# Loading the second weight slab in halves and asking for the rotary and bias tables behind it, at the entry of a long kernel

## The chip, the cores and the metric

The kernel runs on one core of one Trainium2 chip. The time is device microseconds of one execution of the whole program; lower is better. A core has a matrix engine (TensorE, PE in the profile; its weight loads are PEld), a vector engine (DVE), a scalar engine (ACT), GpSimd (POOL), a sequencer for DMA (SP), and 16 DMA engines that all queues share.

## What is computed

The reference is a chain of residual layers on 256 tokens of width 1024, in float32. Two layers of a first model (axial-rotary grouped-query attention beside dilated attention with a bias table, then an MLP; latent attention, then an MLP) are followed by two of a second model (gated MLP, differential attention, gated MLP; gated MLP, retention, gated MLP). Only the entry of the first layer matters here:

```python
hn = rms_norm(h, norm_mix_g[0])
proj = hn @ ab_w_in[0]
qa, ka, va, qb, kb, vb = jnp.split(proj, split_ab, axis=-1)
qa = rms_norm(qa.reshape(b, s, A_HEADS, HEAD_DIM), a_q_norm_g[0])
ka = rms_norm(ka.reshape(b, s, A_KV_HEADS, HEAD_DIM), a_k_norm_g[0])
qa = apply_rope(qa, cos_ax, sin_ax)
ka = apply_rope(ka, cos_ax, sin_ax)
...
biases.append(rel_bias[t5_bucket(off)].astype(jnp.float32).T)
```

## The kernel before

Weights come from memory as slabs of 128 x 2048 float32 (1 MB). The ring `raw` holds six of them. SP asks for slab n + 6 once slab n has been split. The split turns a slab into a high part `whi` (a cast by ACT, `split_high`, L241) and a low part `wlo` (raw minus high, by DVE, `split_low`, L245), each with a ring of three. The activations are split in the same way into `xh` and `xl`, both in the tile `xhl`. A product is then three matmuls: high with high, high with low, low with high. TensorE takes the slabs in the order in which they lie in memory. Every engine's program is written out by hand, and only semaphores tie the engines together, so each engine runs its list strictly in order.

The entry of the kernel:

- **SP** (L2675 to L2680) asks for the first 128 rows of x, the first half of slab 0, the other 128 rows of x, the second half of slab 0, then slabs 1 to 5 whole.
- **ACT** (`raw_scalar`, q = 0) casts the first half of slab 0, scales a block of transposed x (`first_side`), casts the second half, scales two more blocks, casts slab 1 whole (L241), and then squares x for the norm (L510). Before all of that, at L2781, it asks for the rotary table `tabs` (128 x 256, 128 KB) once the first rows of x have landed.
- **DVE** (`norm_vector`, q = 0) makes the low parts of x (`first_rest`, L549) and of the halves of slab 0 (`first_low`, L233), then the low part of slab 1 (L245).
- **TensorE** transposes x (L498), multiplies with slab 0 in pieces (`first_block`, L395), then with slab 1 (`second_slab`): for each half t of the tokens, 16 matmuls with the high part of the slab (L430, L431), behind a wait for `hi_ready`, and 8 with the low part (L434), behind a wait for `lo_ready`. Next are the bias table (`table_tensor`, L1381, which waits for `rel_loaded`), a spread of the norm factors (L754), slab 2 (`project_tokens`, L260 to L262), and after its first 24 matmuls the transposition of the rotated keys (`turn_kind(0)`, L1039), which waits for DVE's `ab_roped`.
- **POOL** asks for the gains of the rotary table (`rope_rows`, L2702, which land in `tabs` too) when the first rows of x have landed, and for the bias tables when the second have: `rel_sb` (L2704, 16 KB), `hot_sb` (L2706, 64 KB, part of tile sub_rstd), `cnt_sb` (L2707, 256 KB, tile sub_o). It then multiplies table by gains, four times (L2711), which gives `rope_ready`.
- DVE waits for `rope_ready` ahead of `roped(0)` (L1267 to L1292), the norm and rotation of the keys, behind the low part of slab 2 (L245) and a sum (L1259).

Of the kernel before, what the change touches and what calls it, by code (L numbers as in the profile page):

```python
# [23 lines left out]
F32 = mybir.dt.float32  # L24
F32R = mybir.dt.float32r
BF16 = mybir.dt.bfloat16
ALU = mybir.AluOpType
# [4 lines left out]
T = 256  # L32
TB = T // P
D = 1024
KC = D // P
SLAB = 2048
IN_W = SLAB // KC
OUT_K = SLAB // D
RAW = 6
# [70 lines left out]
C_TAB = C_CNT + REL  # L110
# [14 lines left out]
def program(nc, weights, x, gains, columns, consts, rel_bias, lam, rope_gain, scratch, out):  # L125
    with ExitStack() as ctx:
# [18 lines left out]
        tabs = sb("tabs", [P, 2048])  # L145
# [62 lines left out]
        def S(name):  # L208

            if name not in SEMS:  # L210
                SEMS[name] = sem(name)
            return SEMS[name]

        def W(part, n, k, lo, hi, width=IN_W):

            return part[:, n % SPLIT, k * width + lo:k * width + hi]


        def first_high(act, part):
            half = slice(part * SLAB // 2, (part + 1) * SLAB // 2)  # L220
            if part == 0:
                act.wait_ge(S("first_half"), 16)
            else:
                act.wait_ge(raw_loaded[0], 16)
            nc.scalar.copy(whi[:, 0, half], raw[:, 0, half]).then_inc(S("first_half") if part == 0 else hi_ready, 1)

        def first_low(dve, part):
            half = slice(part * SLAB // 2, (part + 1) * SLAB // 2)
            if part == 0:
                dve.wait_ge(S("first_half"), 17)  # L230
            else:
                dve.wait_ge(hi_ready, 1)
            nc.vector.tensor_tensor(wlo[:, 0, half], raw[:, 0, half], whi[:, 0, half].bitcast(F32),  # L233
                                    ALU.subtract).then_inc(S("first_half") if part == 0 else lo_ready, 1)

        def split_high(act, m, i=None):

# [151 lines left out]
        def first_block(pe, bank):  # L389


            def part(t, first, sides):
                for k in range(first, first + 4):
                    act, weight = (xl if sides == "lh" else xh), (wlo if sides == "hl" else whi)
                    mm = nc.tensor.matmul(bank[:, t * T:(t + 1) * T], act[:, k, t * P:(t + 1) * P],  # L395
                                          W(weight, 0, k, 0, T), start=k == 0 and sides == "hh",
                                          stop=k == KC - 1 and sides == "hl")
                return mm

            turn_block(pe, 0, 0)  # L400
            pe.wait_ge(xh_ready, 1)
            pe.wait_ge(S("first_half"), 17)
# [4 lines left out]
            pe.wait_ge(S("first_half"), 18)  # L407
            part(0, 0, "hl")
            pe.wait_ge(xh_ready, 2)
            pe.wait_ge(hi_ready, 1)  # L410
            part(0, 4, "hh")
            pe.wait_ge(xl_ready, 2)
            part(0, 4, "lh")
            pe.wait_ge(lo_ready, 1)
            part(0, 4, "hl")
            for half in range(2):
                pe.wait_ge(xh_ready, 3 + half)
                part(1, 4 * half, "hh")
                pe.wait_ge(xl_ready, 3 + half)
                part(1, 4 * half, "lh")  # L420
                mm = part(1, 4 * half, "hl")
            return mm

        def second_slab(pe, n, bank):

            for t in range(TB):
                dst = bank[:, t * T:(t + 1) * T]
                pe.wait_ge(hi_ready, n + 1)
                for k in range(KC):
                    nc.tensor.matmul(dst, xh[:, k, t * P:(t + 1) * P], W(whi, n, k, 0, T), start=k == 0, stop=False)  # L430
                    nc.tensor.matmul(dst, xl[:, k, t * P:(t + 1) * P], W(whi, n, k, 0, T), start=False, stop=False)  # L431
                pe.wait_ge(lo_ready, n + 1)
                for k in range(KC):
                    mm = nc.tensor.matmul(dst, xh[:, k, t * P:(t + 1) * P], W(wlo, n, k, 0, T), start=False,  # L434
                                          stop=k == KC - 1)
            return mm
# [129 lines left out]
        def raw_scalar(act, q, s, n):  # L566

            if q == 0:
                act.wait_ge(mats_loaded, 16)
                first_high(act, 0)  # L570
                act.wait_ge(xh_ready, 1)
                first_side(act, (1,))
                first_high(act, 1)
                first_side(act, (2, 3))
                split_high(act, n + 1)
                for t in range(TB):
                    act.wait_ge(x_loaded[t], 16)
                act.sem_inc(h_ready, len(PIECES))
                for p in range(len(PIECES)):
                    square_piece(act, s, p)  # L580
                return
            else:
                square_piece(act, s, 0)
                square_piece(act, s, 1)
            take_high(act, q, (0, 1, 2))
# [100 lines left out]
        def norm_vector(dve, q, s, n, u=None, factor=1.0):  # L686

            if q == 0:
                dve.wait_ge(mats_loaded, 16)
                dve.wait_ge(turned, 1)  # L690
                nc.vector.tensor_tensor(xh[:, 0:4, 0:P], up[0][:, :].rearrange("p (c n) -> p c n", c=4),
                                        first_cols[:, 0:4].unsqueeze(2).broadcast_to([P, 4, P]), ALU.mult
                                        ).then_inc(xh_ready, 1)
                first_rest(dve, (0,))
                first_low(dve, 0)
                first_rest(dve, (1,))
                first_low(dve, 1)
                first_rest(dve, (2, 3))
                dve.sem_inc(xn_ready, len(PIECES))
                split_low(dve, n + 1)  # L700
                raw_stats(dve, s)
                return
            split_low(dve, n)
            add_piece(dve, u, 0, n, factor)
            gain_piece(dve, q, s, 0)
            add_piece(dve, u, 1, n, factor)
            gain_piece(dve, q, s, 1)
            if q == FINAL_Q:
                final_gained(dve, 1)
# [1963 lines left out]
        @block.sync  # L2673
        def _(sp):
            sp.dma_start(h[:, 0, :], x[0, 0:P, :]).then_inc(x_loaded[0], 16)  # L2675
            sp.dma_start(raw[:, 0, 0:SLAB // 2], weights[0][:, 0:SLAB // 2]).then_inc(S("first_half"), 16)
            sp.dma_start(h[:, 1, :], x[0, P:T, :]).then_inc(x_loaded[1], 16)
            sp.dma_start(raw[:, 0, SLAB // 2:SLAB], weights[0][:, SLAB // 2:SLAB]).then_inc(raw_loaded[0], 16)
            for n in range(1, RAW):
                sp.dma_start(raw[:, n, :], weights[n]).then_inc(raw_loaded[n], 16)  # L2680
            turns = SLABS // RAW - 1
            with sp.Fori(0, turns) as i:
# [15 lines left out]
        def _(pool):  # L2698
            nc.gpsimd.memset(zero[:, :], 0.0).then_inc(filled, 1)
            nc.gpsimd.memset(eps[:, :], EPS).then_inc(filled, 1)  # L2700
            pool.wait_ge(x_loaded[0], 16)
            pool.dma_start(rope_rows[:, :], rope_gain.broadcast_to([P, 4 * HD])).then_inc(S("rope_rows"), 16)  # L2702
            pool.wait_ge(x_loaded[1], 16)
            pool.dma_start(rel_sb[:, :].rearrange("p (c h) -> p c h", h=B_HEADS),  # L2704
                           rel_bias.unsqueeze(1).broadcast_to([NB, COPIES, B_HEADS])).then_inc(S("rel_loaded"), 16)
            pool.dma_start(hot_sb, consts[0:NB, C_HOT:C_HOT + REL]).then_inc(S("rel_loaded"), 16)  # L2706
# [69 lines left out]
        def _(act):  # L2776
            act.dma_start(first_in[:, :], columns[:, G_ALL:G_ALL + KC + P]).then_inc(mats_loaded, 16)
            act.wait_ge(filled, 2)
            bring_table(ACT.Sqrt)
            act.wait_ge(x_loaded[0], 16)  # L2780
            act.dma_start(tabs[:, 0:T], consts[:, C_TAB:C_TAB + T]).then_inc(S("rope_loaded"), 16)  # L2781
            raw_scalar(act, 0, 0, FIRST["ab_in"])
            ab_scalar(act)
            norm_scalar(act, 1, 1, FIRST["mlp0"])
# [247 lines left out]
```

## Time and profile before

| | |
|---|---|
| time, median of 3 runs | 1609.76 us (1609.74 to 1609.76) |
| profiled execution, its own time | 1610.46 us |
| span of its instructions | 1608.4 us |
| TensorE busy | 1601.1 us, x8645 matmuls |
| DVE busy | 1050.6 us |
| ACT busy | 852.7 us |
| POOL busy | 45.7 us |
| granted TensorE clock, mean | 1.000 |
| bytes moved | 294.26 MB, mean 183 GB/s |

TensorE is busy nearly all the time. Its idle time lies almost all at the very start. The profiled execution is 0.70 us over the median, and 2.06 us of it lie outside the span.

### The profile page before, as it was taken

How to read it: one execution, taken by the hardware profiler on the slowest of the kernel's cores; microseconds unless marked ns; L12 is line 12 of the kernel's file. 1: busy time of each engine (PE TensorE's matmuls, PEld its weight loads, DVE VectorE, ACT ScalarE, POOL GpSimd, SP SyncE). 2: the span in 40 equal slices, each digit the busy share in tenths (PEclk: the TensorE clock that was granted, in tenths of full speed). 3: DMA queues.
4: the chain of work that ended last, by engine and by line, in shares of the span. 5: the costliest groups of instructions: out<-in, count | busy, mean ns of one | idle time of the engine just before them, and what ended most of it. 6: DMA issues, size and time to landing. Idle time of an engine off the chain costs nothing.

```text
span 1608.4 us, 22435 instructions
## 1 busy us (share of the span) xinstructions
PE 1601.1 (100%) x8645; PEld 1353.1 (84%) x8645; DVE 1050.6 (65%) x1215; ACT 852.7 (53%) x1069; POOL 45.7 (3%) x50
## 2 busy tenths in 40 slices
PE   9999999999999999999999999999999999999999
PEld 7878888978888888888888888888888888888887
DVE  6866656877656776667777666766667554566665
ACT  6654444785444554446776444554445554554453
POOL 2100000000000030000100000000000000000000
PEclk9999999999999999999999999999999999999999
DMA  9635455524555465445345555455455444445540
GB/s 354 229 119 216 178 207 185 167 104 168 200 207 186 154 222 202 189 181 186 132 169 197 209 183 186 167 209 203 189 180 199 164 176 174 166 156 192 202 183 26
DMA packets 42854, 294.26 MB, mean 183 GB/s; under 512 B 4784, under 2 KB 5344, under 8 KB 8736
## 3 DMA queue, kind: packets, MB, share of 16 engines
q1 hardware_dynamic: 39312, 281.04, 47.5%
q0 software_dynamic: 3184, 12.02, 2.3%
q8 instruction: 52, 0.85, 0.2%
q10 hardware_dynamic: 288, 0.20, 0.0%
q14 instruction: 18, 0.15, 0.0%
HBM read 289.18 MB, written 3.15 MB: 182 GB/s over the span
## 4 chain that ended last, share of the span: by engine, by line
PE 98%; DMA 1%; DVE 1%; ACT 0%; issue 0%; SPq 0%; DVEq 0%
PE ups L293 26%; PE accs L260 15%; PE accs L261 15%; PE accs L262 15%; PE ups L296 13%; PE accs L293 2%; PE ups L498 1%; PE accs L296 1%; PE ups L1448 1%; PE accs L449 1%; PE accs L446 1%; PE accs L451 1%; DMA raw<-weights 1%; PE ups L2501 1%; PE ups L1069 1%; PE ups L1058 1%
## 5 line engine op out<-in xcount | busy, mean ns | idle before, releaser
L245 DVE TENSOR_TENSOR wlo<-raw,whi 128x2048 fp32r<-128x2048 f32 x263 | 603.9, 2299 | 214.9 <-ACT whi L241 214.7
L293 PE MATMUL ups<-xhl,whi 128*128 128x512 f32 x1824 | 572.8, 395 | 0.0
L241 ACT CAST whi<-raw 128x2048 fp32r<-128x2048 f32 x265 | 505.5, 1910 | 106.1 <-PE accs L262 105.1
L296 PEld LDWEIGHTS ups<-xhl,wlo 128*128 128x128 f32 x1824 | 342.6, 188 | 80.3
L296 PE MATMUL ups<-xhl,wlo 128*128 128x256 f32 x1824 | 358.3, 278 | 0.0
L293 PEld LDWEIGHTS ups<-xhl,whi 128*128 128x128 f32 x1824 | 282.4, 189 | 5.0
L260 PE MATMUL accs<-whi,hidh 128*128 128x512 f32 x692 | 272.2, 393 | 0.0
L261 PE MATMUL accs<-wlo,hidh 128*128 128x512 f32 x692 | 269.7, 390 | 0.0
L262 PE MATMUL accs<-whi,hidl 128*128 128x512 f32 x692 | 269.4, 389 | 0.0
L262 PEld LDWEIGHTS accs<-whi,hidl 128*128 128x128 f32 x692 | 129.9, 188 | 27.7
L260 PEld LDWEIGHTS accs<-whi,hidh 128*128 128x128 f32 x692 | 129.9, 188 | 24.3 <-issue 0.7
L261 PEld LDWEIGHTS accs<-wlo,hidh 128*128 128x128 f32 x692 | 130.0, 188 | 23.2
L260 PE MATMUL accs<-whi,xhl 128*128 128x512 f32 (+1 forms) x352 | 139.1, 395 | 0.3 <-DVE xhl L2307 0.3
L262 PE MATMUL accs<-whi,xhl 128*128 128x512 f32 (+1 forms) x352 | 134.0, 381 | 0.0
L261 PE MATMUL accs<-wlo,xhl 128*128 128x512 f32 (+1 forms) x352 | 133.8, 380 | 0.0
L894 DVE TENSOR_TENSOR hid<-ups,hid 128x512 f32<-128x512 f32 x70 | 48.3, 691 | 118.6 <-ACT hid L865 67.1
L873 ACT CAST hidh<-hid 128x512 fp32r<-128x512 f32 x76 | 47.2, 621 | 128.0 <-DVE hid L918 75.7
L865 ACT COPY hid<-ups 128x512 f32<-128x512 f32 x40 | 23.4, 586 | 130.0 <-PE ups L296 130.0
L920 DVE TENSOR_TENSOR hidl<-hid,hidh 128x512 fp32r<-128x512 f32 x76 | 52.6, 692 | 52.2 <-ACT hidh L873 52.2
L260 PEld LDWEIGHTS accs<-whi,xhl 128*128 128x128 f32 x352 | 66.3, 188 | 14.3 <-issue 3.2
L262 PEld LDWEIGHTS accs<-whi,xhl 128*128 128x128 f32 x352 | 66.2, 188 | 13.1
L261 PEld LDWEIGHTS accs<-wlo,xhl 128*128 128x128 f32 x352 | 66.4, 189 | 12.1 <-issue 1.0
(274 smaller groups left out, 1401.9 us busy)
## 6 DMA issues: line engine op xcount, KB each, us to landing
raw<-weights SPq DMA_DIRECT2D x265, 1024.0 KB, 4.8
gain<-gains POOLq DMA_DIRECT2D x9, 512.0 KB, 4.0
rel_scratch<-sub_rstd POOLq DMA_DIRECT2D x1, 2048.0 KB, 9.9
big<-rel_scratch POOLq DMA_DIRECT2D x1, 1536.0 KB, 7.8
h<-x_in SPq DMA_DIRECT2D x2, 512.0 KB, 5.2
raw<-weights SPq DMA_DIRECT2D x2, 512.0 KB, 6.6
tabs<-consts POOLq DMA_DIRECT2D x1, 1024.0 KB, 6.5
big<-big POOLq DMA_DIRECT2D x2, 384.0 KB, 4.8
```

Of the source, the lines that this page charges most:

```text
L241: nc.scalar.copy(whi[:, m % SPLIT, :], raw[:, m % RAW, :]).then_inc(hi_ready, 1)
L245: nc.vector.tensor_tensor(wlo[:, m % SPLIT, :], raw[:, m % RAW, :], whi[:, m % SPLIT, :].bitcast(F32), ALU.subtract).then_inc(lo_ready, 1)
L260: nc.tensor.matmul(out_ap, sh, mh, start=first, stop=False)
L261: nc.tensor.matmul(out_ap, sh, ml, start=False, stop=False)
L262: return nc.tensor.matmul(out_ap, sl, mh, start=False, stop=last)
L293: mm = nc.tensor.matmul(bank, W(whi, n, k, j * P, (j + 1) * P), xhl[:, k, :, :].rearrange("p a n -> p (a n)"), start=k == 0, stop=False)
L296: mm = nc.tensor.matmul(bank[:, 0:T], W(wlo, n, k, j * P, (j + 1) * P), xh[:, k, :], start=False, stop=k == KC - 1)
L446: mm = nc.tensor.matmul(bank, W(whi, n, k, j * P, (j + 1) * P), xl[:, k, :], start=False, stop=k == KC - 1)
L865: nc.scalar.copy(flat2(slot), first_parts if begin else sum_parts(0)[1]).then_inc(S("feed_side"), 1)
L873: nc.scalar.copy(hidh[:, g % per, :, :].rearrange("p a n -> p (a n)"), slot).then_inc(S("feed_hidden_high"), 1)
L894: nc.vector.tensor_tensor(flat2(part), sum_parts(second)[0], flat2(part), ALU.add).then_inc(S("feed_sum"), 1)
L920: nc.vector.tensor_tensor(hidl[:, g % per, :, :].rearrange("p a n -> p (a n)"), slot, hidh[:, g % per, :, :].rearrange("p a n -> p (a n)") ...
```

## The change

The split of slab 1 is made like that of slab 0: SP asks for it in two halves, ACT casts it in two halves, DVE subtracts in two halves, and TensorE waits for each half apart. The semaphore `half1` counts the first half (16 for the load, then 17 for its high part and 18 for its low part), and `raw_loaded[1]`, `hi_ready` and `lo_ready` the second. The request for the rotary table moves on ACT from the head of the program to behind the two casts. On POOL the request for the rotary gains waits for the first half of slab 1 instead of the first rows of x, and those for the bias tables wait for its second half instead of the second rows of x. Everything else is as before.

```diff
-        def first_high(act, part):
+        def half_of(part):
+            return slice(part * SLAB // 2, (part + 1) * SLAB // 2)
+
+        def first_high(act, m, part):
+            act.wait_ge(S(f"half{m}") if part == 0 else raw_loaded[m], 16)
+            nc.scalar.copy(whi[:, m, half_of(part)], raw[:, m, half_of(part)]
+                           ).then_inc(S(f"half{m}") if part == 0 else hi_ready, 1)
+
+        def first_low(dve, m, part):
...
+                dve.wait_ge(S(f"half{m}"), 17)
             else:
-                dve.wait_ge(hi_ready, 1)
...
+                dve.wait_ge(hi_ready, m + 1)
...
             for t in range(TB):
                 dst = bank[:, t * T:(t + 1) * T]
-                pe.wait_ge(hi_ready, n + 1)
+                pe.wait_ge(S("half1"), 17)
                 for k in range(KC):
+                    if k == KC // 2:
+                        pe.wait_ge(hi_ready, n + 1)
...
-                pe.wait_ge(lo_ready, n + 1)
+                pe.wait_ge(S("half1"), 18)
                 for k in range(KC):
+                    if k == KC // 2:
+                        pe.wait_ge(lo_ready, n + 1)
...
-                split_high(act, n + 1)
+                first_high(act, 1, 0)
+                first_high(act, 1, 1)
+                act.dma_start(tabs[:, 0:T], consts[:, C_TAB:C_TAB + T]).then_inc(S("rope_loaded"), 16)
...
-                split_low(dve, n + 1)
+                first_low(dve, 1, 0)
+                first_low(dve, 1, 1)
...
-            for n in range(1, RAW):
+            sp.dma_start(raw[:, 1, 0:SLAB // 2], weights[1][:, 0:SLAB // 2]).then_inc(S("half1"), 16)
+            sp.dma_start(raw[:, 1, SLAB // 2:SLAB], weights[1][:, SLAB // 2:SLAB]).then_inc(raw_loaded[1], 16)
+            for n in range(2, RAW):
...
-            pool.wait_ge(x_loaded[0], 16)
+            pool.wait_ge(S("half1"), 16)
             pool.dma_start(rope_rows[:, :], rope_gain.broadcast_to([P, 4 * HD])).then_inc(S("rope_rows"), 16)
-            pool.wait_ge(x_loaded[1], 16)
+            pool.wait_ge(raw_loaded[1], 16)
...
-            act.wait_ge(x_loaded[0], 16)
-            act.dma_start(tabs[:, 0:T], consts[:, C_TAB:C_TAB + T]).then_inc(S("rope_loaded"), 16)
             raw_scalar(act, 0, 0, FIRST["ab_in"])
```

On ACT, at the entry, where the whole cast of slab 1 stood (L241, behind the last block of x) ahead of the squares (L510), the list before is:

```order
12 L538 ACTIVATE xhl<-ups,first_in 128x128 x3
13 L241 CAST whi<-raw 128x2048 [waits raw_loaded1]
14 L510 ACTIVATE big,ssq<-h 128x1024 [waits x_loaded0,x_loaded1,h_ready]
15 L510 ACTIVATE big,ssq<-h 128x512 [waits h_ready] x2
16 L596 ACTIVATE std<-mean_eps 128x2 [waits half_ready]
```

and in the changed kernel:

```order
11 L542 ACTIVATE xhl<-ups,first_in 128x128 x3
12 L224 CAST whi<-raw 128x1024 [waits half1]
13 L224 CAST whi<-raw 128x1024 [waits raw_loaded1]
14 L581 DMA tabs<-consts 128x256
15 L514 ACTIVATE big,ssq<-h 128x1024 [waits x_loaded0,x_loaded1,h_ready]
16 L514 ACTIVATE big,ssq<-h 128x512 [waits h_ready] x2
17 L602 ACTIVATE std<-mean_eps 128x2 [waits half_ready]
```

The one cast has become two of half the width, and the request for the rotary table, which was row 4 of the list, now stands between them and the squares.

On POOL, the requests for the tables and the products behind them before:

```order
8 L2702 DMA tabs<-rope_gain 128x256 [waits x_loaded0]
9 L2704 DMA rel_sb<-rel_table 32x16x8 [waits x_loaded1]
10 L2706 DMA sub_rstd<-consts 32x512
11 L2707 DMA sub_o<-consts 128x512
12 L2711 ISA
13 L2711 TENSOR_TENSOR big<-tabs 128x128 [waits rope_loaded,rope_rows]
```

and in the changed kernel:

```order
8 L2711 DMA tabs<-rope_gain 128x256 [waits half1]
9 L2713 DMA rel_sb<-rel_table 32x16x8 [waits raw_loaded1]
10 L2715 DMA sub_rstd<-consts 32x512
11 L2716 DMA sub_o<-consts 128x512
12 L2720 ISA
13 L2720 TENSOR_TENSOR big<-tabs 128x128 [waits rope_loaded,rope_rows]
```

Nothing has changed places; only what the first two requests wait for is different.

## Rows read from the trace of the kernel before

**Rows 1.** The page: busy time by engine, and the chain that ended last by engine.

```profile
PE 1601.1 (100%) x8645; PEld 1353.1 (84%) x8645; DVE 1050.6 (65%) x1215; ACT 852.7 (53%) x1069; POOL 45.7 (3%) x50
...
PE 98%; DMA 1%; DVE 1%; ACT 0%; issue 0%; SPq 0%; DVEq 0%
```

**Rows 2.** Chain that ended last, 0 to 60 us: start us, us, what.

```profile
2.60 11.07 DMA raw<-weights
13.69 1.92 ACT whi L241
15.63 2.30 DVE wlo L245
17.97 1.22 PE accs L434 x8
...
22.07 1.05 PE ups L1381 x2
...
26.63 0.22 PE accs L1039 x2
```

**Rows 3.** Timeline of PE: start us, us, engine line op, xcount, [idle before].

```profile
15.04 0.64 PE L395 MATMUL accs<-wlo,xhl 128*128 128x256 f32 x4
15.65 0.39 PE L430 MATMUL accs<-whi,xhl 128*128 128x256 f32 x1
15.87 0.28 PE L431 MATMUL accs<-whi,xhl 128*128 128x256 f32 x1
...
17.54 0.28 PE L431 MATMUL accs<-whi,xhl 128*128 128x256 f32 x1
...
19.03 0.28 PE L430 MATMUL accs<-whi,xhl 128*128 128x256 f32 x1
```

**Rows 4.** Timeline of ACT.

```profile
9.62 1.05 ACT L225 CAST whi<-raw 128x1024 fp32r<-128x1024 f32 x1 [0.54 <-DMA raw<-weights]
...
10.58 2.17 ACT L538 ACTIVATE xhl<-ups,first_in 128x128 fp32r<-128x128 f32 x8
...
15.50 1.05 ACT L510 ACTIVATE big<-h 128x1024 f32<-128x1024 f32 x1
```

**Rows 5.** Timeline of DVE.

```profile
10.70 1.23 DVE L233 TENSOR_TENSOR wlo<-raw,whi 128x1024 fp32r<-128x1024 f32 x1 [0.37 <-ACT whi L225]
11.85 2.15 DVE L549 SCALAR_TENSOR_TENSOR xhl<-ups,first_in,xhl 128x128 fp32r<-128x128 f32 x8
...
23.38 0.17 DVE L1267 RECIPROCAL rstd<-std 128x4 f32<-128x4 f32 x1
...
24.91 0.42 DVE L1292 TENSOR_TENSOR big<-big 128x256 f32<-128x256 f32 x1
```

**Rows 6.** Timeline of ACT's queue and of POOL: requests, and the rotary products.

```profile
4.55 0.34 ACTq L2781 DMA_DIRECT2D tabs<-consts  x1
...
8.58 0.70 POOL L2704 DMA_DIRECT2D rel_sb<-rel_table  x1 [3.07 <-DMA h<-x_in]
...
9.79 0.58 POOL L2707 DMA_DIRECT2D sub_o<-consts  x1
...
13.14 1.73 POOL L2711 TENSOR_TENSOR big<-tabs 128x128 f32<-128x128 f32 x4 [2.78 <-DMA tabs<-consts]
```

**Rows 7.** DMA requests, 0 to 60 us: KB each, median us from request to landing.

```profile
sub_o<-consts POOLq DMA_DIRECT2D x1, 256.0 KB, 8.0
tabs<-consts ACTq DMA_DIRECT2D x1, 128.0 KB, 8.5
tabs<-rope_gain POOLq DMA_DIRECT2D x1, 128.0 KB, 7.2
```

**Rows 8.** DMA queues, 9 to 10 us: packets, MB, share of 16 engines.

```profile
q0 software_dynamic: 24, 0.10, 80.0%
...
q10 hardware_dynamic: 25, 0.03, 7.2%
```

**Rows 9.** Windows: engines' busy (x), granted clock, DMA share, GB/s.

```profile
12.00:13.00 1.00, 1.00 (x9) 1.00 (x8) 1.00 (x5) 0.74 (x3) 0.00 (x0) 1.00 1.04 433
```

More of the change, by code:

```diff
@@ L216, in W @@
             return part[:, n % SPLIT, k * width + lo:k * width + hi]
-        def first_high(act, part):
-            half = slice(part * SLAB // 2, (part + 1) * SLAB // 2)
+        def half_of(part):
[5 more added lines that the diff above has]
+        def first_low(dve, m, part):
             if part == 0:
-                act.wait_ge(S("first_half"), 16)
+                dve.wait_ge(S(f"half{m}"), 17)
             else:
[L224 to L231, printed above, removed]
-                dve.wait_ge(hi_ready, 1)
-            nc.vector.tensor_tensor(wlo[:, 0, half], raw[:, 0, half], whi[:, 0, half].bitcast(F32),
-                                    ALU.subtract).then_inc(S("first_half") if part == 0 else lo_ready, 1)
+                dve.wait_ge(hi_ready, m + 1)
+            nc.vector.tensor_tensor(wlo[:, m, half_of(part)], raw[:, m, half_of(part)],
+                                    whi[:, m, half_of(part)].bitcast(F32),
+                                    ALU.subtract).then_inc(S(f"half{m}") if part == 0 else lo_ready, 1)
         def split_high(act, m, i=None):
@@ L401, in first_block @@
             pe.wait_ge(xh_ready, 1)
-            pe.wait_ge(S("first_half"), 17)
+            pe.wait_ge(S("half0"), 17)
             part(0, 0, "hh")
@@ L406, in first_block @@
             turn_block(pe, 0, 1)
-            pe.wait_ge(S("first_half"), 18)
+            pe.wait_ge(S("half0"), 18)
             part(0, 0, "hl")
@@ L569, in raw_scalar @@
                 act.wait_ge(mats_loaded, 16)
-                first_high(act, 0)
+                first_high(act, 0, 0)
                 act.wait_ge(xh_ready, 1)
                 first_side(act, (1,))
-                first_high(act, 1)
+                first_high(act, 0, 1)
                 first_side(act, (2, 3))
-                split_high(act, n + 1)
+                first_high(act, 1, 0)
+                first_high(act, 1, 1)
+                act.dma_start(tabs[:, 0:T], consts[:, C_TAB:C_TAB + T]).then_inc(S("rope_loaded"), 16)
                 for t in range(TB):
@@ L694, in norm_vector @@
                 first_rest(dve, (0,))
-                first_low(dve, 0)
+                first_low(dve, 0, 0)
                 first_rest(dve, (1,))
-                first_low(dve, 1)
+                first_low(dve, 0, 1)
                 first_rest(dve, (2, 3))
                 dve.sem_inc(xn_ready, len(PIECES))
-                split_low(dve, n + 1)
+                first_low(dve, 1, 0)
+                first_low(dve, 1, 1)
                 raw_stats(dve, s)
@@ L2675, in _ @@
             sp.dma_start(h[:, 0, :], x[0, 0:P, :]).then_inc(x_loaded[0], 16)
-            sp.dma_start(raw[:, 0, 0:SLAB // 2], weights[0][:, 0:SLAB // 2]).then_inc(S("first_half"), 16)
+            sp.dma_start(raw[:, 0, 0:SLAB // 2], weights[0][:, 0:SLAB // 2]).then_inc(S("half0"), 16)
             sp.dma_start(h[:, 1, :], x[0, P:T, :]).then_inc(x_loaded[1], 16)
             sp.dma_start(raw[:, 0, SLAB // 2:SLAB], weights[0][:, SLAB // 2:SLAB]).then_inc(raw_loaded[0], 16)
-            for n in range(1, RAW):
+            sp.dma_start(raw[:, 1, 0:SLAB // 2], weights[1][:, 0:SLAB // 2]).then_inc(S("half1"), 16)
+            sp.dma_start(raw[:, 1, SLAB // 2:SLAB], weights[1][:, SLAB // 2:SLAB]).then_inc(raw_loaded[1], 16)
+            for n in range(2, RAW):
                 sp.dma_start(raw[:, n, :], weights[n]).then_inc(raw_loaded[n], 16)
```

## The prediction

> **What bounds the kernel now.** Read the page first: TensorE is busy 1601.1 of 1608.4 us, and the chain of work that ended last lies on it for 98% [rows 1]. So an edit at the entry can move the end only by the time that TensorE waits there. The chain from 0 to 60 us shows these waits [rows 2]: it is one DMA up to 13.67 us (the load of slab 1, asked for at 2.60), then ACT's cast of the slab (1.92), then DVE's subtraction (2.30), and from 17.97 on TensorE without a break up to the bias table at 22.07 and the transposition of the keys at 26.63. The timelines of PE, ACT, DVE and POOL then show what each engine had in hand. The rate of TensorE is one 128x256 matmul in 0.12 us: from 15.87 to 17.54 there are 14 steps [rows 3]. The granted clock is at its higher level, 2.4 GHz, throughout.
>
> **What TensorE loses.** Four matmuls of slab 0 begin at 15.04, so the fifth place is at 15.52 and the sixth at 15.64. The second matmul of slab 1 begins at 15.87 instead [rows 3], as the high part came at 15.6. That is 0.23 us. After the high part's 16 matmuls the next place is 17.54 + 0.12 = 17.66, and eight matmuls with the low part would end in 18.62. The next one after them begins at 19.03 [rows 3], since the low part was ready only at 17.93 [rows 2]. That is 0.41 us. Together 0.64 us, and this is all that halving slab 1 can give by itself.
>
> **Halving the slab.** ACT is through with x at 10.58 + 2.17 = 12.75 [rows 4]. A half cast takes 1.05 [rows 4], so the high part is complete near 14.8, against TensorE's 15.5. DVE is through with x at 14.00, and a half subtraction takes 1.23 [rows 5]: low halves at 15.2 and 16.4 against TensorE's 17.4. Both waits of TensorE go. The load need not even be quicker: if the second half landed at 13.67 as the whole did, its cast would start on time within 0.1. One instruction more on ACT and one on DVE cost 0.18 and 0.16 (2 x 1.05 against 1.92, 2 x 1.23 against 2.30), which these 0.7 and 1.0 us of cover hide. The four waits more on TensorE are found fulfilled; I take 0, with 0.1 as the upper end, as the wait for `hi_ready` ahead of the second 16 matmuls leaves no gap in the chain. SP issues one request more, ahead of slabs 2 to 5, which no one waits for. What is late next is slab 0 itself, not slab 1.
>
> **Moving the requests: what it gives.** From 9 to 10 us the software queue held the DMA engines for 80.0% of their time for 0.10 MB, and ACT's queue for 7.2% more [rows 8]. These are the rotary gains and the rotary table, in the very microsecond in which the second half of slab 0 ends and slab 1 begins. Without them the rate is 433 GB/s [rows 9], so slab 1 (1.05 MB) needs 2.4 us behind 9.6: its halves land at 10.8 and 12.0. TensorE has no use for that, but the tables are asked for by it. The second half of slab 0 may gain too. Its cast waited until 9.62 [rows 4], and it sets the whole rest of `first_block` through DVE's L233 at 10.70. DVE sat idle 0.37 before that [rows 5], so 0.37 is the most that it can give, and nothing the least. I take 0.1, nearer to nothing, because the tables had only begun to move when that half ended. TensorE would reach the bias table at 22.07 - 0.64 - 0.1 = 21.3 and the keys at 26.63 - 0.74 = 25.9.
>
> **Moving the requests: what it costs, bias table.** POOL asks for `rel_sb` at 12.0 instead of 8.58, and for `cnt_sb` 9.79 - 8.58 = 1.21 later [rows 6], at 13.2. From request to landing it took 8.0 [rows 7], so 21.2, against 21.3 for TensorE: no wait, with 0.1 to spare. If the second half lands at 13.67 as the slab does now, it is 22.9 and TensorE waits 1.6; by 11.7 or sooner nothing is near. I take no wait: the row is for the same bytes on the same queue.
>
> **Moving the requests: what it costs, rotary table.** Here the cover was large (POOL's products were over at 13.14 + 1.73 = 14.87, DVE asked at 23.38 [rows 5, 6]) and nearly all of it goes. ACT asks for the table behind two casts, near 14.5 instead of 4.55. It took 8.5 to land [rows 7], which gives 23.0. Part of that was time behind the gains of the software queue (80% of a microsecond, [rows 8]), which now will have landed at 10.8 + 7.2 = 18.0 [rows 7]; against that, the 256 KB of `cnt_sb` now move at the same time, 0.6 us at 433 GB/s, shared among queues. I take 7.9, between 7.2 (the quickest table of this size) and 8.5 + 0.6 = 9.1: landing at 22.4. POOL's four products take 1.73 and begin 0.1 later: 24.2. DVE, which is free near 23.0 (the squares on ACT start some 0.4 earlier), waits, and then needs 24.91 + 0.42 - 23.38 = 1.95 up to the rotated keys [rows 5]: 26.15. TensorE stands there at 25.9, waits 0.25, and is still 26.63 - 26.15, so some 0.5 us, ahead of before. By 7.2 DVE is done at 25.45, TensorE doesn't wait, and the gain is the whole 0.74. By 9.1 it is done at 27.35, and the kernel is 0.7 slower. The waits don't add up: only the later of the two chains counts. DVE's next wait in `roped(1)` is for TensorE's transposition itself, so lateness is paid once. Queued behind POOL's products are `cols`, `lamb` and the store of the bias table, which waits for a result of DVE that comes long after.
>
> What is behind 27 us shifts as a block: TensorE waits for nothing long there, and engines off the path wait for it.
>
> The Trainium skill, page "DMA: Bandwidth & Descriptors", section "Anatomy of one DMA", gives a transfer's time as some 2.0 us fixed and its bytes at 436 GB/s. For the 128 KB table that is an estimate of 2.3 us and not 8.5. By that rule the table would be there at 16.8, no wait would be left, and the sum would be the full gain, 1609.0; but this trace's row for the same request says 8.5, as the queues are full of slabs, and I go by the row.
>
> **Sum.** 0.23 + 0.41 + 0.1 - 0.25 = 0.5 us. The profiled execution took 1610.46, so it would take 1609.96 with the change; the median of the runs is 0.70 under it, and the forecast is 1609.76 - 0.5, so 1609.3.
>
> **Rivals.**
> - *The table is quick* (7.2 us or less, a mechanism of its own: nothing but slabs ahead of it). TensorE never waits: 0.74 less, 1609.0. For it: the gains were in its way before. Against it: all three requests on rows 7 took 7 us or more. Chance 0.20.
> - *The table is late* (slower). ACT's request lands more than 8.4 us after 14.5, DVE ends the keys behind 26.63, and TensorE waits over 0.74. Between 0.1 and 0.9 slower, 1610.2. For it: the row is 8.5, and `cnt_sb` comes on top. Against it: what held the table up before is gone by then. Chance 0.17.
> - *Bias table late, or gain absorbed.* Slab 1's second half lands after 12.6 and TensorE waits for `rel_loaded` until 21.9 or 22.1. It is then where it was: 1609.8, give or take 0.2. This is also the change not doing what it says, the slab not coming sooner. Chance 0.13.
> - *More than forecast.* Slab 0's second half comes 0.3 earlier, and the tables are in time: 0.9 to 1.1 less, 1608.7. Chance 0.10.
> - Something not seen, beyond 3 us either way: 0.05.
>
> **How the numbers follow.** The forecast (a gain of 0.3 to 0.65) has 0.35, the largest share: 1609.3. To hold eight in ten the range takes it, the quick table, half of the larger gain, the absorbed case and somewhat over half of the late table: 0.35 + 0.20 + 0.05 + 0.13 + 0.10, so 0.83, from 1608.7 to 1610.2. A measurement of this kernel can tell about 0.2% from no change, which is 3.2 us; all the named cases lie inside it. That leaves 0.03 for faster, 0.95 for the same and 0.02 for slower.
>
> **What would show it.** In the trace of the changed kernel: slab 1's high casts at 12.7 and 13.7 on ACT; PE's matmuls of slab 1 at 0.12 each with no idle time; the bias table's matmul at 21.3; POOL's rotary products from 22.4 to 24.2, and DVE idle for them between 23 and 24; the keys' transposition near 26.2. Wrong would be: an idle PE ahead of the bias table (then the third rival), products of POOL that begin before 21.8 (the first) or after 23.0 (the second), or a stretch behind 27 us that doesn't keep the distance.

## The result, and the profile after

The changed kernel takes 1614.20 us in the median of 8 runs (1612.62 to 1616.75), the kernel before 1609.86 in 8 runs beside it (1609.74 to 1610.63). The ratio is 1.0027, with a 95% interval of 1.0016 to 1.0038: slower by 0.27%. The forecast was 1609.3, in a range of 1608.7 to 1610.2. Not only the middle is new but the spread: 4.1 us from the fastest to the slowest, against 0.9 before. On the whole, the slower a run, the lower its mean granted clock: 1.000 at 1612.62, 0.999 at 1613.38, 1613.88, 1614.22 and 1614.27, 0.998 at 1614.18 and 1615.88, 0.997 at 1616.75.

The profiled execution is the fastest one, 1612.62 us with a span of 1610.6. That is 2.16 over the profiled execution before (1610.46). The page, as [rows 1]:

```profile
PE 1600.5 (99%) x8645; PEld 1352.7 (84%) x8645; DVE 1051.2 (65%) x1216; ACT 852.7 (53%) x1070; POOL 45.4 (3%) x50
...
PE 97%; DMA 1%; DVE 1%; ACT 0%; issue 0%; SPq 0%; POOL 0%; DVEq 0%
```

TensorE is busy no longer than before, so the extra time is idle time. The chain that ended last, 0 to 60 us (start us, us, what), answers to [rows 2]:

```profile
3.35 8.58 DMA raw<-weights
11.93 0.30 issue
12.23 0.70 POOL rel_sb L2713
12.92 0.50 POOL sub_rstd L2715
13.43 10.25 DMA sub_o<-consts
23.72 1.12 PE ups L1388 x2
...
28.36 0.22 PE accs L1046 x2
```

The cast and the subtraction of slab 1 are gone from the chain. In their place stands the load of `cnt_sb`, the 256 KB table: asked for at 13.43, landed at 23.68. The bias table's matmul begins at 23.72 instead of 22.07, and the keys' transposition at 28.36 instead of 26.63. TensorE's own rows, as [rows 3] (start us, us, line, op, count, idle time before):

```profile
20.09 1.12 PE L438 MATMUL accs<-wlo,xhl 128*128 128x256 f32 x8
23.72 0.69 PE L1388 MATMUL ups<-sub_rstd,rel_sb 32*128 32x512 f32 x1 [2.52 <-DMA sub_o<-consts]
```

Slab 1 ends at 21.2, and then 2.52 us pass idle. Engines and queues around it, as [rows 4], [rows 5] and [rows 6]:

```profile
11.96 0.34 ACTq L581 DMA_DIRECT2D tabs<-consts  x1
...
12.35 2.04 ACT L224 CAST whi<-raw 128x1024 fp32r<-128x1024 f32 x2
```

```profile
10.96 0.69 POOL L2711 DMA_DIRECT2D tabs<-rope_gain  x1 [9.66 <-DMA raw<-weights]
12.23 0.70 POOL L2713 DMA_DIRECT2D rel_sb<-rel_table  x1 [0.58 <-DMA raw<-weights]
...
13.43 0.58 POOL L2716 DMA_DIRECT2D sub_o<-consts  x1
22.79 1.69 POOL L2720 TENSOR_TENSOR big<-tabs 128x128 f32<-128x128 f32 x4 [8.79 <-DMA tabs<-consts]
```

```profile
24.52 0.18 DVE L1274 RECIPROCAL rstd<-std 128x4 f32<-128x4 f32 x1 [1.96 <-POOL big L2720]
```

And how long the tables took to land, as [rows 7] (KB, median us to landing):

```profile
sub_o<-consts POOLq DMA_DIRECT2D x1, 256.0 KB, 10.3
tabs<-rope_gain POOLq DMA_DIRECT2D x1, 128.0 KB, 6.3
tabs<-consts ACTq DMA_DIRECT2D x1, 128.0 KB, 10.7
```

Why 10.3 instead of 8.0: the DMA queues of the changed kernel from 16.5 to 17.5 us, and from 17 to 18 us (packets, MB, share of 16 engines by queue), beside [rows 8]:

```profile
q0 software_dynamic: 19, 0.02, 170.5%
```

```profile
DMA packets 10, 0.01 MB, mean 10 GB/s; under 512 B 0, under 2 KB 10, under 8 KB 10
```

Nineteen packets of the software queue, 0.02 MB in all, hold the sixteen engines for 1.7 us. Fifteen of them belong to the 16 KB of `rel_sb`, which moves in sixteen packets of 1 KB (the first begins at 16.28) and is read sixteen times over in pieces of 32 bytes. For the microsecond from 17 to 18 next to nothing moves on any queue. In the kernel before a weaker stall fell on the rotary gains, from 9.3 us on (eleven packets took 0.60 to 0.95 us each), and nothing waited for the gains.

### The profile page after: what moved, and what is told of

It is laid out like the page before. It is cut to its first block, busy times and chain, and to the rows that moved or that the text cites. A ratio compares the mean times of both kernels' runs of the same rounds, so it can differ in the third digit from the quotient of the medians.

```text
span 1610.6 us, 22438 instructions
## 1 busy us (share of the span) xinstructions
PE 1600.5 (99%) x8645; PEld 1352.7 (84%) x8645; DVE 1051.2 (65%) x1216; ACT 852.7 (53%) x1070; POOL 45.4 (3%) x50
## 4 chain that ended last, share of the span: by engine, by line
PE 97%; DMA 1%; DVE 1%; ACT 0%; issue 0%; SPq 0%; POOL 0%; DVEq 0%
PE ups L293 26%; PE accs L260 15%; PE accs L262 15%; PE accs L261 15%; PE ups L296 13%; PE accs L293 2%; PE ups L502 1%; PE accs L296 1%; PE ups L1455 1%; PE accs L453 1%; PE accs L450 1%; PE accs L455 1%; PE ups L2508 1%; DMA sub_o<-consts 1%; PE ups L1076 1%; DMA raw<-weights 1%
## 5 line engine op out<-in xcount | busy, mean ns | idle before, releaser
L241 ACT CAST whi<-raw 128x2048 fp32r<-128x2048 f32 x264 | 503.6, 1910 | 105.4 <-PE accs L262 105.4
```

The lines of the kernel that those rows point to most:

```text
L241: nc.scalar.copy(whi[:, m % SPLIT, :], raw[:, m % RAW, :]).then_inc(hi_ready, 1)
```

## Where the 4.3 us are, first reading

TensorE's matmuls can be matched one by one, since both kernels have 8645 of them in nearly the same order. The shift of each in the changed kernel against its start before, in the two profiled executions (by PE's timeline, where the bias table's matmul of the kernel before starts at 22.00; the chain has 22.07):

| | shift, us |
|---|---|
| last matmul of slab 1 | -0.88 |
| bias table | +1.72 |
| 700th matmul, near 111 us | +1.72 |
| 710th matmul | +2.10 |
| last matmul | +2.15 |

Two losses, then: 2.6 us ahead of the bias table (from a lead of 0.88), and 0.38 near 112 us. They make up the fastest run. The other runs have 0.8 to 4.1 us more, with a lower mean clock.

**Theory A:** TensorE waits for the 256 KB table, and in most runs its clock is lowered behind the idle time. **B:** halving slab 1 costs something itself. **C:** the rotary table is what is waited for. **D:** the runs differ because the table lands at different times, and the clock is only a companion.

## One part of the change at a time

**Halves only.** The requests are put back:

```diff
-            pool.wait_ge(S("half1"), 16)
+            pool.wait_ge(x_loaded[0], 16)
...
-            pool.wait_ge(raw_loaded[1], 16)
+            pool.wait_ge(x_loaded[1], 16)
...
-                act.dma_start(tabs[:, 0:T], consts[:, C_TAB:C_TAB + T]).then_inc(S("rope_loaded"), 16)
...
+            act.wait_ge(x_loaded[0], 16)
+            act.dma_start(tabs[:, 0:T], consts[:, C_TAB:C_TAB + T]).then_inc(S("rope_loaded"), 16)
```

> Slab 1 in halves; all table requests where they were before. Theory A (the loss is TensorE's 2.5 us wait for the bias table, and in most runs a lower clock behind it): no wait for the tables, 0.6 to 0.8 under the kernel before, so 1609.0 to 1609.2, with the runs within 0.9 of each other as for the kernel before. Theory B (halving costs: the extra waits, or the 0.4 us that DVE loses near 112 us in the changed kernel): 1610.2 or more. Theory C (the late rotary table): as A here.

Measured: 1610.09 (1609.96 to 1611.14, 11 runs), ratio 1.0001 (0.9992 to 1.0010). No table is waited for. In the profiled execution TensorE is 0.74 us ahead at the end of slab 1 (the last group begins at 20.21 instead of 20.95), which is the 0.64 I had worked out and 0.1 more, and is 0.73 ahead at 111 us; then it gives back 0.38. The time is nearly 1 us over the 1609.0 to 1609.2 of theory A; the 0.38 are part of that. Halving is harmless and gains 0.36 in the profiled execution (1610.10 against 1610.46), which the medians of this kernel don't show. The loss is in the requests.

**Requests only.** Slab 1 whole again, all requests behind it:

```diff
-            pool.wait_ge(x_loaded[0], 16)
+            pool.wait_ge(raw_loaded[1], 16)
...
-            pool.wait_ge(x_loaded[1], 16)
+            pool.wait_ge(raw_loaded[1], 16)
...
                 split_high(act, n + 1)
+                act.dma_start(tabs[:, 0:T], consts[:, C_TAB:C_TAB + T]).then_inc(S("rope_loaded"), 16)
...
-            act.wait_ge(x_loaded[0], 16)
-            act.dma_start(tabs[:, 0:T], consts[:, C_TAB:C_TAB + T]).then_inc(S("rope_loaded"), 16)
```

> Slab 1 whole; the requests for the rotary table, the rotary gains and the bias tables behind it. Theory A: the wait of 2 to 3 us on TensorE ahead of the bias table stays, 1612 to 1615 with runs that differ by 1 us or more. Theory B: at most 1609.9.

Measured: 1614.67 (1614.10 to 1616.81, 6 runs), ratio 1.0032 (1.0020 to 1.0044). TensorE's waits of this kernel (engine line waited for: us in total, times, longest us):

```profile
PE ups L1382 <- DMA sub_o<-consts: 3.3, 1, 3.3
```

Theory B is out: without halves the loss is the same. This profile shows more. Slab 1 landed whole at 11.70 instead of 13.66, as the requests no longer moved beside it, and TensorE was 1.03 us ahead at its end (19.92 instead of 20.95) without any halves. So each part of the change removes the waits for slab 1 by itself, and with the requests moved the halves add nothing to be seen. And behind the wait for the table TensorE loses 1.5 us more in the next 16 matmuls or so of slab 2, as they follow each other at twice the distance. The windows of the kernel (columns as [rows 9]; the granted clock is the number ahead of the DMA share):

```profile
24.00:26.00 2.00, 1.65 (x5) 0.90 (x6) 1.86 (x8) 1.63 (x1) 0.86 (x2) 0.90 1.01 422
26.00:28.00 2.00, 2.00 (x12) 2.00 (x11) 0.63 (x1) 0.00 (x0) 0.00 (x0) 0.50 1.00 407
28.00:30.00 2.00, 2.00 (x15) 2.00 (x15) 0.00 (x0) 0.00 (x0) 0.00 (x0) 0.75 1.02 406
30.00:32.00 2.00, 2.00 (x19) 2.00 (x18) 1.16 (x3) 0.38 (x1) 0.00 (x0) 1.00 0.96 401
```

From 25.6 on, 1.2 us after the 3.3 us of idle time ended, the granted clock is at its lower level, 1.2 GHz (0.50), for some 3.4 us, in which TensorE does half of what it would. That is the second half of the loss.

**Bias tables early, rotary table late.**

```diff
+            pool.wait_ge(x_loaded[1], 16)
+            pool.dma_start(rel_sb[:, :].rearrange("p (c h) -> p c h", h=B_HEADS),
+                           rel_bias.unsqueeze(1).broadcast_to([NB, COPIES, B_HEADS])).then_inc(S("rel_loaded"), 16)
+            pool.dma_start(hot_sb, consts[0:NB, C_HOT:C_HOT + REL]).then_inc(S("rel_loaded"), 16)
+            pool.dma_start(cnt_sb, consts[:, C_CNT:C_CNT + REL]).then_inc(S("rel_loaded"), 16)
             pool.wait_ge(S("half1"), 16)
             pool.dma_start(rope_rows[:, :], rope_gain.broadcast_to([P, 4 * HD])).then_inc(S("rope_rows"), 16)
-            pool.wait_ge(raw_loaded[1], 16)
...
```

> The changed kernel with the bias tables asked for as before, when the second rows of x have landed; only the rotary table and its gains are late. Theory A: no wait ahead of the bias table's matmul, 1609.0 to 1609.4, narrow spread. Theory C (the late rotary table holds DVE and through it TensorE): 1611 or more, with an idle TensorE ahead of the transposition of the keys.

Measured: 1610.33 (1610.07 to 1614.06, 11 runs), ratio 1.0002 (0.9993 to 1.0011). Ten runs lie between 1610.07 and 1610.97, one at 1614.06, and that one is the profiled execution. In it the rotary table took 12.2 us to land, and TensorE waited for the keys. The 256 KB table took 11.5 us from its early request at 9.77, so it landed at 21.27, just as TensorE came to it.

```profile
26.04 0.18 DVE L1274 RECIPROCAL rstd<-std 128x4 f32<-128x4 f32 x1 [3.49 <-POOL big L2720]
```

```profile
28.05 0.57 PE L1046 MATMUL accs<-first_in,big 128*128 128x128 f32 x2 [2.11 <-DVE big L1299]
```

So theory A holds for the usual run: with the bias tables early the 4 us are gone, though the median is still 0.9 above the 1609.4 that I had allowed. But the late rotary table, my own term for a loss, is real too: in one run of eleven it was over its edge, with the lower clock behind it. How near the other ten came is not shown, as there is no profile of them.

**Rotary table early, bias tables late.**

```diff
-            pool.wait_ge(S("half1"), 16)
+            pool.wait_ge(x_loaded[0], 16)
             pool.dma_start(rope_rows[:, :], rope_gain.broadcast_to([P, 4 * HD])).then_inc(S("rope_rows"), 16)
             pool.wait_ge(raw_loaded[1], 16)
...
-                act.dma_start(tabs[:, 0:T], consts[:, C_TAB:C_TAB + T]).then_inc(S("rope_loaded"), 16)
...
+            act.wait_ge(x_loaded[0], 16)
+            act.dma_start(tabs[:, 0:T], consts[:, C_TAB:C_TAB + T]).then_inc(S("rope_loaded"), 16)
```

> The changed kernel with the rotary table and its gains asked for as before; only the bias tables are late. Theory A: TensorE still waits for the 256 KB table, though less if that table lands sooner without the rotary table beside it (8.0 us instead of 10.25 would leave 0.3 of wait): 1609.5 to 1613. Theory C: 1609.1.

Measured: 1615.75 (1614.27 to 1616.21, 7 runs), ratio 1.0031 (1.0020 to 1.0043), 2.75 above the top of what I had expected of theory A. The 256 KB table did land sooner after its request, in 9.2 us. But the request itself came 2.1 us later (POOL's timeline), since with the rotary requests early slab 1's second half landed at 13.99 instead of 11.93, and TensorE waited 3.6 us:

```profile
14.29 0.70 POOL L2712 DMA_DIRECT2D rel_sb<-rel_table  x1 [8.56 <-DMA raw<-weights]
14.98 0.52 POOL L2714 DMA_DIRECT2D sub_rstd<-consts  x1
15.49 0.58 POOL L2715 DMA_DIRECT2D sub_o<-consts  x1
```

```profile
24.75 1.22 PE L1387 MATMUL ups<-sub_rstd,rel_sb 32*128 32x512 f32 x1 [3.62 <-DMA sub_o<-consts]
```

The granted clock then stayed low for longer (windows of this kernel):

```profile
22.00:24.00 2.00, 0.00 (x0) 0.00 (x0) 1.93 (x5) 2.00 (x4) 0.00 (x0) 0.90 1.02 399
24.00:26.00 2.00, 1.25 (x2) 0.50 (x2) 1.77 (x6) 1.72 (x1) 0.00 (x0) 0.50 1.02 416
26.00:28.00 2.00, 2.00 (x7) 1.26 (x7) 0.00 (x0) 0.00 (x0) 0.00 (x0) 0.50 1.02 426
28.00:30.00 2.00, 2.00 (x11) 2.00 (x11) 0.00 (x0) 0.00 (x0) 0.00 (x0) 0.50 0.99 414
```

The shift of TensorE goes from 2.75 at the bias table to 5.34 at the keys: 2.6 us for the clock alone. Theory C, for which this kernel should have been at 1609.1, is out as the main cause.

## Is it the idle time that lowers the clock?

Filler matmuls on a tile of zeros were put where TensorE waits. They only add work.

```diff
+            stay_warm(7)
             table_tensor(pe)
```

> The changed kernel with seven matmuls on a tile of zeros (128x512 in bf16, 0.43 us each at the start of the program, so 3.0 us) ahead of the bias table's matmul, where TensorE waited 2.5 us. They can only add work. Theory A (the clock of TensorE falls behind the idle time and costs 1 to 4 us in most runs): the granted clock is 1.000 in all runs, the time 1612.6 to 1613.4 with a spread under 1 us, so faster than the changed kernel by about 1 us in spite of more work. Theory D (the runs differ because the 256 KB table lands at different times, the clock being an effect and no cause): the spread stays at 2 us or more and the median is no lower than 1614.

Measured: 1614.60 (1612.87 to 1615.17, 7 runs), ratio 1.0027 (1.0016 to 1.0038). By the numbers that I had set, this is theory D: a spread of 2.3 us, a median not under 1614, a clock of 0.999 in all seven runs. But it does not decide, as the fillers were too short. The six that the profile shows begin and end within 1.46 us. I had read 0.43 us for each at the start of the program, where TensorE runs at half the rate: in the kernel before, the first eight transpositions of x, at 5.12, took 1.83 us, and the next eight, at 9.21, took 1.03. So 1.93 us of idle time were left behind the fillers, and in the profiled execution the clock fell:

```profile
21.32 1.46 PE L352 MATMUL ups<-zero 128*128 128x512 bf16 x6
24.71 1.12 PE L1389 MATMUL ups<-sub_rstd,rel_sb 32*128 32x512 f32 x2 [1.93 <-DMA sub_o<-consts]
```

With enough of them:

```diff
+            stay_warm(17)
             table_tensor(pe)
```

> The changed kernel with 17 matmuls on zeros ahead of the bias table's matmul; in e5 each took 0.21 us and seven ended 1.9 us before the table landed, so these end near 24.9 and leave no idle time there. Theory A: the clock never falls behind them; the granted clock is 1.000 in nearly all runs, the time 1613.6 to 1614.4 with a spread of about 1 us, against 1612.6 to 1616.8 without fillers. Theory D: the spread stays at 3 us or more, clocks down to 0.997.

Measured: 1613.78 (1613.62 to 1614.80, 10 runs), ratio 1.0025 (1.0015 to 1.0034). Seven runs lie within 0.2 us of each other and three near 1614.7; the profiled one (1613.73) has a granted clock of 1.000. The three slower ones have 0.999, and what lowered their clock is open. There is no idle time left in front of the bias table:

```profile
21.30 3.62 PE L352 MATMUL ups<-zero 128*128 128x512 bf16 x16
24.85 1.12 PE L1389 MATMUL ups<-sub_rstd,rel_sb 32*128 32x512 f32 x2
```

TensorE is held until 24.85, 1.1 us longer than in the profile of the changed kernel. Still the slowest run is 1.95 us under the slowest of the changed kernel, and the fastest is 1.0 over its fastest. The fillers hide two things at once, the idle time and any difference in when the table lands up to 24.85. The second can't be all: then the changed kernel's runs would end where these do, at 1613.6 to 1614.8 or under, and two of its eight are at 1615.88 and 1616.75. The clock's own figure agrees: at a mean of 0.997 a run of 1615 us has lost 0.003 x 1615 = 4.8 us, give or take 0.8 for the rounding, and that run is 4.1 over the fastest.

But the second isn't small either. Four kernels make their requests for tables alike and differ only on TensorE, and in their profiled executions the 256 KB table landed at 23.68 (the changed kernel), 24.03 (seventeen fillers), 24.66 (seven fillers) and 25.36 (the next experiment). So theory A stands, with a part of D in it. Of the 4.34 us between the medians, 2.16 are wait and hesitation, as between the two profiled executions; 1.58 is what the median run lies over the fastest one, with the lower clock in it and perhaps a later landing, which these runs don't separate; and 0.60 is what the profiled execution before lay over its own median.

## What makes the table late

**The bias table's matmul moved behind the keys.**

```diff
-            table_tensor(pe)
...
             turn_kind(1)
+            table_tensor(pe)
             piece(3, 0)
```

> The changed kernel with the bias table's matmul taken behind the second transposition (keys and first queries) instead of ahead of slab 2, so TensorE doesn't wait for the 256 KB table. Theory A: the wait for it goes; the rotary table is next, since its products end at 24.5 and the keys are ready at 26.5: TensorE waits there some 1.5 to 2 us and the time is 1610.5 to 1611.5. Theory C' (the rotary table would be in time too once DMA is no longer waited for): 1609.2.

Measured: 1614.20 (1611.66 to 1615.95, 11 runs), ratio 1.0023 (1.0014 to 1.0032). The wait for the 256 KB table is gone and the wait for the rotary table has taken its place, longer than I had expected (3.61 in the profiled execution, 1.5 to 2 expected; the time is 2.7 over the upper end of 1610.5 to 1611.5). The rotary table took 13.2 us to land. This profile, one of the slowest runs, shows the clock low twice: from 8 to 11 us, behind 1.74 us of waiting for slab 0's high part, and again around the wait for the keys, from 28.4 on:

```profile
7.91 2.04 PE L395 MATMUL accs<-whi,xhl 128*128 128x256 f32 x8 [1.74 <-ACT whi L224]
29.03 0.69 PE L1046 MATMUL accs<-first_in,big 128*128 128x128 f32 x2 [3.61 <-DVE big L1299]
```

```profile
9.00:10.00 1.00, 1.00 (x7) 1.00 (x7) 1.00 (x5) 0.59 (x1) 0.00 (x0) 0.50 1.07 438
...
30.00:31.00 1.00, 1.00 (x6) 1.00 (x6) 1.00 (x3) 0.13 (x1) 0.00 (x0) 0.50 1.02 411
```

In this kernel the two tables stand one behind the other: with the first wait removed TensorE meets the second. With the bias tables asked for early, above, that shows in one run of eleven.

**Only the small table early.**

```diff
+            pool.wait_ge(x_loaded[1], 16)
+            pool.dma_start(rel_sb[:, :].rearrange("p (c h) -> p c h", h=B_HEADS),
+                           rel_bias.unsqueeze(1).broadcast_to([NB, COPIES, B_HEADS])).then_inc(S("rel_loaded"), 16)
             pool.wait_ge(S("half1"), 16)
...
-            pool.dma_start(rel_sb[:, :].rearrange("p (c h) -> p c h", h=B_HEADS),
-                           rel_bias.unsqueeze(1).broadcast_to([NB, COPIES, B_HEADS])).then_inc(S("rel_loaded"), 16)
```

> The changed kernel with only the 16 KB bias table (read sixteen times over in pieces of 32 bytes) asked for as before; the gains, the hot rows and the 256 KB table stay late. In the changed kernel its 16 packets held the DMA engines 1.8 us each. Theory G (these packets, moving beside the rotary table, are what made the 256 KB table 2 us later than I had reckoned): no packet of it over 0.3 us, the 256 KB table lands 8 to 8.5 us after its request, TensorE waits at most 0.5 us for it: 1609.8 to 1611. Theory H (the stall falls on whatever the software queue holds then): other packets of that queue take 0.6 us or more, and the wait stays at 1.5 us or more: 1612 or more.

Measured: 1611.41 (1610.88 to 1614.75, 11 runs), ratio 1.0011 (1.0002 to 1.0020). The median lies between the theories, nearer to G: 2.8 us of the loss are gone. But the profiled execution (1614.75, the slowest) looks like H. Five of the small table's sixteen packets took 0.83 to 3.41 us, from 12.8 us on, ten packets of the queue's other tables 0.63 to 1.06 us, and the 256 KB table took 11.5 us:

```profile
PE ups L1388 <- DMA sub_o<-consts: 3.0, 1, 3.0
```

So the stall isn't bound to the small table. All thirteen profiles have one, with packets of the software queue that took over 0.6 us, within some 1.5 us after that queue begins to move: on the gains where these are asked for with the first rows of x, and first of all on the small table where the gains come later. Asking for the small table early did not keep it out. What sets it off stays open.

**The requests behind slab 0.**

```diff
-            pool.wait_ge(S("half1"), 16)
+            pool.wait_ge(raw_loaded[0], 16)
             pool.dma_start(rope_rows[:, :], rope_gain.broadcast_to([P, 4 * HD])).then_inc(S("rope_rows"), 16)
-            pool.wait_ge(raw_loaded[1], 16)
...
                 first_high(act, 0, 1)
+                act.dma_start(tabs[:, 0:T], consts[:, C_TAB:C_TAB + T]).then_inc(S("rope_loaded"), 16)
...
-                act.dma_start(tabs[:, 0:T], consts[:, C_TAB:C_TAB + T]).then_inc(S("rope_loaded"), 16)
```

> Slab 1 in halves, and the requests for all the tables behind slab 0 instead of slab 1 (9.4 us instead of 11 to 12.2 on POOL, 9.4 instead of 12.0 on ACT). Theory A: bias tables land by 20.8, ahead of TensorE at 21.2, the rotary products end by 22: hardly a wait, 1609.3 to 1610.3. Theory I (the tables take 2 us more to land than before wherever they are put behind the first rows): TensorE waits 1 us or more, 1611 or more.

Measured: 1611.31 (1610.84 to 1615.57, 11 runs), ratio 1.0012 (1.0003 to 1.0021). In its profiled execution (1613.83) the 256 KB table was asked for at 11.44, two microseconds sooner than in the changed kernel, and took 12.0 us:

```profile
sub_o<-consts POOLq DMA_DIRECT2D x1, 256.0 KB, 12.0
```

The median is above the 1610.3 of theory A and in the range of theory I. Where the three requests stand is not what decides, though. Laid side by side, the profiled executions part by the rotary requests. In the five kernels that ask for the rotary table and its gains with the first rows of x, the 256 KB table took 8.0, 8.4, 9.1, 9.2 and 9.5 us. In the eight that ask for them later it took 10.3 to 12.0. The 9.2 is the kernel whose bias tables are late, and the two of 11.5 are the kernels that ask early for all three bias tables or for the small one. So, by one profiled execution of each, the 2.3 us more in the changed kernel go with the rotary table and gains that move beside the 256 KB table. How much of it is the stall of 1.7 us and how much the sharing of engines is not shown.

## The 0.38 us at 112 us

The changed kernel gives back 0.38 near 112 us, and so does the one with halves only. VectorE begins an addition there (L743 before) later after the same event. It has one instruction more ahead of it than before. Two kernels test that, each with one more on VectorE where it is idle:

```diff
+                nc.vector.tensor_scalar(pad[:, :], first_cols[:, 0:1], 0.5, None, ALU.mult)
                 raw_stats(dve, s)
...
+        pad = sb("pad", [P, 1])
```

> The kernel before with the same instruction of 128x1 more on VectorE. Theory E: VectorE hesitates near 110 us as in e1, TensorE loses 0.3 there: 1610.3. Theory F: no loss, 1610.0.

Added to the kernel before: 1610.40 (1610.12 to 1610.88, 11 runs), ratio 1.0003 (0.9994 to 1.0012). The shift of TensorE goes from -0.41 to -0.03 between the 700th and the 710th matmul: the 0.38 appear in a kernel without halves. VectorE's row, with the idle time before it:

```profile
109.06 1.23 DVE L744 SCALAR_TENSOR_TENSOR h<-accs,h 128x1024 f32<-128x1024 f32 x1 [2.83 <-PE accs L262]
```

> Slab 1 in halves, requests as before (as in e1), and one instruction of 128x1 more on VectorE at the entry, where it has nothing to do. In e1 TensorE was 0.72 us ahead until 112 us and gave back 0.30 there, where VectorE begins an addition 0.45 us after the semaphore event that frees it instead of 0.07. Theory E (this hesitation hangs on the number of instructions ahead of it in VectorE's program): it is gone or elsewhere, and the lead of 0.7 stays: 1609.4 to 1609.8. Theory F (it comes from the halves themselves): 1610.1 as e1.

Added to the kernel with halves only: 1610.53 (1609.75 to 1610.99, 11 runs), ratio 1.0003 (0.9994 to 1.0012). Here the 0.38 are gone at that place (-0.29 and -0.28), and the same row reads:

```profile
108.80 1.23 DVE L750 SCALAR_TENSOR_TENSOR h<-accs,h 128x1024 f32<-128x1024 f32 x1 [2.47 <-PE accs L262]
```

The idle time is 2.47 with two added instructions (2.45 with none, in the kernel before and in the one with requests only) and 2.83 with one (2.82 with halves only, 2.83 in the changed kernel). All ten kernels with 1216 instructions on VectorE lose 0.38 at this place, and the three with 1215 or 1217 don't. But this kernel had lost 0.54 at slab 2 already, where VectorE began a subtraction 0.42 later than with halves only, and loses 0.36 again further on. Its time, 1610.53, is over both expectations. Theory E holds for the place and not for the sum: where the hesitation falls hangs on the number of instructions, and in this kernel hesitations take the whole of a lead of 0.82 us. What VectorE does in that time no row shows.

## Why the prediction was wrong, point by point

- **What TensorE loses at slab 1, and that halving removes it: right.** The forecast was a lead of 0.64 from halving and 0.1 from slab 0; it was 0.88 in the changed kernel and 0.74 with halves only. Slab 0's second cast began at 9.39, so 0.23 sooner where I took 0.1, and all of that came through (slab 0's last matmuls start at 14.80 instead of 15.04). What I missed is that the moved requests alone remove the same waits: with slab 1 whole the lead was 1.03.
- **Rotary table: the mechanism right.** It was asked for at 11.96 and not 14.5: the request left ACT's queue 0.03 us after the second half of slab 1 had landed (11.93), when the casts ahead of it in the list were still to be done. It took 10.7 us where I took 7.9 and at most 9.1. The two errors cancel: the products began at 22.79 (forecast 22.4) and DVE waited for them until 24.52 (forecast 24.2). In the profiled execution this cost TensorE nothing, as it was late already. The 2.3 us that the prediction sets beside it, from the Trainium skill (page "DMA: Bandwidth & Descriptors", section "Anatomy of one DMA"), are worked out from a fit that the page gives for requests of GpSimd, and this one is ACT's. In the thirteen profiles this request took 7.8 to 13.2 us.
- **Bias table: the step that failed.** I took "no wait: the row is for the same bytes on the same queue". The request came 0.2 later than forecast (13.43), and the landing 10.25 us after it instead of 8.0; TensorE waited 2.5 us. The sum had 0.1 to spare there and gave that term no upper bound on the time to landing, though I gave the rotary table one. I also had the row that warned: 80% of the engines' time for 0.10 MB [rows 8]. I read it as a cost that the old order had and the new one loses. In the changed kernel a stronger stall fell on another table, ahead of one that is waited for, and the rotary requests now moved beside the 256 KB table. How the 2.25 us divide between the two stays open.
- **Granted clock: not in the sum at all.** I wrote that the clock is at its higher level throughout and left it there. (The rate of the first 6 us, half of the later one, speaks against "throughout" too.) A wait on TensorE costs itself, and, in seven of the profiled executions, 1.5 to 2.6 us more around it. Seven of the changed kernel's eight runs have a mean clock under 1.000. The third rival (1609.8, give or take 0.2) had TensorE wait for `rel_loaded`, but as slab 1's second half would land late; it landed at 11.93, as forecast, and the table itself was late.
- **Behind 27 us all shifts as a block: nearly right.** It held to 111 us to within 0.01, then 0.38 were lost to VectorE's hesitation.
- **The chances:** 0.95 for the same rested on all named cases lying inside 3.2 us. The result is outside it by 1.1 us, with a wait that I had priced at 1.6 us at most, and for another reason, and with a factor that I had not priced.

None of the variants is faster than the kernel before: halves only is level with it (1610.09 against 1610.05 in the same session).

## What to carry to other kernels

A load's time from request to landing belongs to what else moves then, not to its bytes and its queue (8.0 to 12.0 us here for the same 256 KB): when a request is moved, give its landing the spread that rows of all loads show, and count the cover that is left against the top of it. A few microseconds saved for a transfer that is not waited for are worth nothing; the cover of 4.2 us that the 256 KB table had before (landed at 17.8, used at 22.0) went with runs within 1 us of each other. And on an engine that sets the time, an idle stretch of two or three microseconds is to be priced with what the granted clock can take on top (1.5 to 2.6 us here), above all where the runs begin to scatter.

## What the runs showed that I had not expected

- Around idle stretches of TensorE of 1.7 to 3.6 us the granted clock went to 1.2 GHz for 3.4 to 6.8 us in the profiled executions of seven kernels; the fall came between 1.1 us before the end of the stretch and 2.2 us after it. It did not fall behind 2.5 us in the changed kernel, nor behind 2.05 us at slab 0 in the kernel with the bias tables early.
- Sixteen packets of 1 KB, read in pieces of 32 bytes, took 1.2 to 2.8 us each and held all DMA engines for some 1.7 us; in the kernel before the same packets took at most 0.05 us.
- A request on ACT's queue left 2.4 us sooner than the compute ahead of it in the program was done, and 0.03 us after the last load that the compute ahead of it waits for.
- One VectorE instruction more at 17 us moves a hesitation of 0.38 us at 109 us in or out.
